# Two merge gates read out by a side branch, and a larger backlog allowed to the RNN steps, in a three-block fp32 transformer kernel

## The reference, cut to what matters

```
h = rms_norm(x, norm_mix_pre)
proj = h @ w_in                                   # 1024 x 6216
xr, gr, q, k, v, iq, ik, iw, g_a, g_b = split(proj)
xc = causal_depthwise_conv(xr, conv_w, conv_b)    # 4 taps
y_rnn = rg_lru(xc, ...) * gelu(gr)                # gates by 64-wide blocks, a scan over the 256 rows
y_a = y_rnn @ w_rnn_out
y_att = dsa_sparse_attention(q, k, v, iq, ik, iw) # 16 heads, the 64 best keys of each row
y_b = y_att @ w_att_out
merged = sigmoid(g_a) * y_a + sigmoid(g_b) * y_b
x = x + rms_norm(merged @ w_o, norm_mix_post)
...                                               # a feed-forward layer, then two more layers
```

## Time and profile before

| what | value |
|---|---|
| median of 3 runs | 1549.5 us |
| lowest and highest of them | 1546.7 and 1559.98 us |
| profiled execution, its own time | 1560.4 us |
| its span, first to last instruction | 1558.6 us |
| PE busy | 1457.6 us, 94% of the span |
| DVE busy | 908.4 us, 58% |
| ACT busy | 742.0 us, 48% |
| mean granted TensorE clock | 0.95 of full |

### The profile page before, as it was taken

How to read it: one execution, slowest core, us unless ns; L and a number is a source line. 1 busy time by engine, 2 the same in 40 slices (tenths; PEclk the granted TensorE clock), 3 DMA queues, 4 the chain that set the end, 5 groups by cost and what they waited for, 6 DMA issues and landing times.

```text
span 1558.6 us, 18397 instructions
## 1 busy us (share of the span) xinstructions
PE 1457.6 (94%) x7100; PEld 1218.9 (78%) x7100; DVE 908.4 (58%) x1445; ACT 742.0 (48%) x1120; POOL 8.1 (1%) x18
## 2 busy tenths in 40 slices
PE   7999799899998999999877999999999929999999
PEld 6898687688887888887656888888888827888887
DVE  5775686565454654547756545555555692565453
ACT  4557674454443544445434444444444525654442
POOL 1000000000000000000000000000000000000000
PEclk9999599999999999999887999999999966999999
DMA  8454055455564556554413565565555420265652
GB/s 264 150 148 122 0 167 185 149 189 178 187 202 149 165 173 202 190 163 150 133 54 100 188 199 176 193 195 180 176 196 190 124 81 1 82 192 172 202 190 68
DMA packets 131767, 242.57 MB, mean 156 GB/s; under 512 B 8544, under 2 KB 21472, under 8 KB 131680
## 3 DMA queue, kind: packets, MB, share of 16 engines
q1 hardware_dynamic: 130768, 239.15, 47.4%
q0 software_dynamic: 624, 2.10, 0.5%
q10 hardware_dynamic: 288, 0.14, 0.0%
HBM read 240.31 MB, written 1.05 MB: 155 GB/s over the span
## 4 chain that ended last, share of the span: by engine, by line
PE 89%; DVE 7%; ACT 2%; issue 1%; DMA 0%; SPq 0%; DVEq 0%
PE PB L449 78%; PE PB L477 3%; PE PB L614 2%; PE PB L679 2%; PE PB L665 1%; PE PB L604 1%; DVE WL L396 1%; DVE SM L536 1%; ACT SR L633 0%; PE PB L1064 0%; DVE SM L522 0%; DVE SM L521 0%; DVE SM L520 0%; DMA X<-in_x_dram 0%; PE PB L578 0%
## 5 line engine op out<-in xcount | busy, mean ns | idle before, releaser
L396 DVE TENSOR_TENSOR WL<-RAW,WH 128x1024 fp32r<-128x1024 f32 (+1 forms) x453 | 534.7, 1213 | 240.3 <-ACT WH L406 240.1
L406 ACT ACTIVATE WH<-RAW 128x1024 fp32r<-128x1024 f32 (+1 forms) x453 | 468.0, 1054 | 331.3 <-PE PB L449 321.1
L449 PE MATMUL PB<-WH,AT0h 128*128 128x512 f32 (+2 forms) x1328 | 510.0, 384 | 16.3 <-DVE WL L396 8.0
L449 PE MATMUL PB<-WL,AT0h 128*128 128x512 f32 (+2 forms) x1328 | 503.3, 379 | 0.0
L449 PE MATMUL PB<-WH,AT0l 128*128 128x512 f32 (+2 forms) x1328 | 502.8, 379 | 0.0
L449 PEld LDWEIGHTS PB<-WH,AT0h 128*128 128x128 f32 x1328 | 255.0, 192 | 64.8 <-ACT AT0h L489 7.0
L449 PEld LDWEIGHTS PB<-WH,AT0l 128*128 128x128 f32 x1328 | 255.0, 192 | 46.1
L449 PEld LDWEIGHTS PB<-WL,AT0h 128*128 128x128 f32 x1328 | 255.3, 192 | 43.3
L449 PE MATMUL PB<-WH,FTh 128*128 128x512 f32 x440 | 174.0, 395 | 0.0
L449 PE MATMUL PB<-WH,FTl 128*128 128x512 f32 x440 | 172.5, 392 | 0.0
L449 PE MATMUL PB<-WL,FTh 128*128 128x512 f32 x440 | 170.8, 388 | 0.0
(11 more groups left out here) (288 smaller groups left out, 1182.8 us busy)
## 6 DMA issues: line engine op xcount, KB each, us to landing
RAW<-in_ffn_w_gu_dram SPq DMA_DIRECT2D x88, 512.0 KB, 4.5
RAW<-in_ffn_w_gu_2b_dram SPq DMA_DIRECT2D x88, 512.0 KB, 4.6
RAW<-in_w_in_dram SPq DMA_DIRECT2D x48, 512.0 KB, 4.0
RAW<-in_ffn_w_down_dram SPq DMA_DIRECT2D x44, 512.0 KB, 4.0
RAW<-in_ffn_w_down_2b_dram SPq DMA_DIRECT2D x44, 512.0 KB, 3.7
RAW<-in_w_ffn_gate_dram SPq DMA_DIRECT2D x22, 512.0 KB, 4.6
RAW<-in_w_ffn_up_dram SPq DMA_DIRECT2D x22, 512.0 KB, 4.7
RAW<-in_w_ffn_down_dram SPq DMA_DIRECT2D x22, 512.0 KB, 4.5
```

What stands on the lines that cost most here:

```text
L396: e.tensor_tensor(o, s, h, ALU.subtract), th, loaded[i], hl_free[i % NHL])
L406: th = op("act", lambda e, o=WH[i % NHL][:, 0:m], s=RAW[i % NRAW][:, 0:m]: e.activation(o, s, ACT.Copy), loaded[i], hl_free[i % NHL])
L449: e.matmul(o, l, r, start=s, stop=p, skip_group_check=feature_major)
```

## The change

It does four things.

1. The read-outs of the four gate products become a generator, `merge_gate`. It is put at the head of `side` and waits there until `conv` (or `gates`) is complete. The main line goes on to the next product at once.
2. Where nothing can go on without the read-outs, the main line waits for all eight of them (`while len(kga) < 4 or len(kgb) < 4`), just ahead of `drain(*rnn_side)`.
3. Since unread gate products now hold banks (two each), `product` first waits, by `onward`, until at least four banks are in the free list. This is in force for all products of the kernel.
4. The RNN's steps wait with `calm(5.0)` in place of `calm(1.5)`, in nine places.

```diff
@@ product
                 nb = n // 128 if feature_major else 2
+                while not carry and len(banks) < 4:
+                    onward()
                 mine = carry or [take() for _ in range(nb // 2 if feature_major else nb)]
@@ rnn, and likewise at its other eight steps
-                    yield from calm(1.5)
+                    yield from calm(5.0)
@@ main line
-            for c in range(2):
-                got_g = product("w_in", 4168 + c * 512, 512, at0, 8)
-                while len(conv) < 4:
-                    onward()
+            def merge_gate(got_g, dst, c, past, toks):
+                while len(past) < 4:
+                    yield
                 for b, (bank, tok) in enumerate(got_g):
-                    kga = op("act", lambda e, b=b, c=c, bank=bank: e.activation(
-                        GA[:, b, c * 512:c * 512 + 512], PB[bank][:, :], ACT.Tanh, scale=0.5), tok, conv)
-                    give(bank, kga)
-            for c in range(2):
-                got_g = product("w_in", 5192 + c * 512, 512, at0, 8)
-                while len(gates) < 4:
-                    onward()
-                for b, (bank, tok) in enumerate(got_g):
-                    kgb = op("act", lambda e, b=b, c=c, bank=bank: e.activation(
-                        GB[:, b, c * 512:c * 512 + 512], PB[bank][:, :], ACT.Tanh, scale=0.5), tok, gates)
-                    give(bank, kgb)
+                    k = op("act", lambda e, b=b, c=c, bank=bank: e.activation(
+                        dst[:, b, c * 512:c * 512 + 512], PB[bank][:, :], ACT.Tanh, scale=0.5), tok, past)
+                    give(bank, k)
+                    toks.append(k)
+
+            kga, kgb = [], []
+            for c0, dst, past, toks in ((4168, GA, conv, kga), (5192, GB, gates, kgb)):
+                for c in range(2):
+                    side.insert(0, merge_gate(product("w_in", c0 + c * 512, 512, at0, 8), dst, c, past, toks))
+            while len(kga) < 4 or len(kgb) < 4:
+                onward()
             drain(*rnn_side)
```

## The result

| | kernel before | changed kernel |
|---|---|---|
| median, runs side by side | 1556.05 us (9 runs) | 1539.35 us (9 runs) |
| lowest and highest | 1546.7 and 1559.98 us | 1535.47 and 1540.71 us |
| profiled execution, its own time | 1560.4 us | 1539.6 us |
| its span | 1558.6 us | 1537.8 us |

The ratio is 0.9896, with a 95% interval of 0.9871 to 0.9921: the change makes the kernel some 16 us faster, by 8 to 13 thousandths (16.7 us by the medians). The forecast was 18.3 us less, from 1549.5 us. With six more runs the median of the kernel before is itself 6.5 us higher than the one that the prediction started from, so the absolute time is 8 us above the forecast, though the step down is nearly as large as forecast.

What follows compares the result with a forecast made beforehand. No engine bounds the bare stretch: two chains run alone while PE's main line stands still, losing 24.3 us. 24.3 - 2.5 - 1.5 - 2 = 18.3 us less than 1549.5 gives 1531.2 us; range 1524 to 1545 us.

Steps and rivals of the forecast that it cites:

- the bare stretch: 151.2 to 192.2 us, nothing dense in PE's queue: waiting and half clock, with the echo behind, lose 24.3 us.
- the read-outs as a branch: Gate products: dense matmuls follow each other, attention's second half moves into `w_rnn_out`, and all 24.3 us can go.
- the larger backlog: RNN steps: convolutions written five chunks earlier; weight copies and attention steps queue behind up to 5 us of RNN work.
- seam term: Between gate products and `w_rnn_out`: RNN's last pair, 29 us, done in time against 36; 1.5 us of waiting (0 to 4).
- the second rival: RNN's last pair late, so the wait returns before `w_rnn_out`: 25 us there, no gain, 1549.5 us within 3; chance 0.08.
- New waits: Three places in the stage where PE would wait instead: 2.5, 1.5 and 2 us, taken off the 24.3 us.
- at the end: Attention's last unit, right ahead of its result's transposes: PE idle in copy and scaling, 2.5 us (1.5 at least, up to 5).
- scattered waits: Small waits all along the stage, where an estimate is a little too early: 2 us, bounds 0.5 and 8.
- the clock case: `w_rnn_out` mixed with attention runs at 1.2 GHz, its 43 us take 86: slower, 1574 us; chance 5%.
- The rest of the span should be the same: Sign for the profile: outside the stage that the change touches, nothing in the span differs.
- carry the difference over as it is: Whole kernel: the median's 10.9 us below the profiled execution kept unexplained, so the forecast starts from 1549.5 us.
- the case of the new waits: Rival: late attention steps stall dense work in `w_rnn_out`, at seam and end; 7 us less, 1542 us (3 to 14); chance 0.20.

Runs made afterwards that it cites:

- The branch alone: Changed kernel with calm(1.5) in place of calm(5.0), read-outs as a branch and guard of four banks kept: 1554.26 us, ratio 1.0002.
- the backlog alone: Kernel before with calm(5.0) in place of calm(1.5) in all nine RNN steps, main line and products as they were: 1539.77 us, ratio 0.9919.
- calm(3.0): Changed kernel with calm(3.0) in place of calm(5.0), branch and guard kept: 1546.6 us, ratio 0.9958.

## Why the prediction was right, and where it was not

**The size of what is lost in the bare stretch: right.** 24.3 us were to go. In the profiles the stage lost 19.5, and 1.8 us of new waits stand in their place; 3.0 us are left. It holds for this execution: in the other two profiles of the kernel before the stage is 2.9 us shorter, so 16.6 us would have gone.

**What removes it: wrong.** "So the PE work of the stretch is unchanged, and all 24.3 us can go" stands under the read-outs as a branch. The branch alone gave a ratio of 1.0002, the backlog alone all of the gain. So the mechanism of the forecast failed, and the right size is in part luck: both parts were in the change, and it made no difference to the sum which of them was named. The step that failed beside it is the one on the larger backlog, "Its cost is that ...": it was costed, and never asked what it gives. The rows of the order had shown it: the last convolution stands five weight chunks earlier on ACT, and it is `calm` that sets where a convolution is written. With `calm(1.5)` my own seam term, "29 us against 36", would have been wrong as well, since the RNN's pair then starts late: the second rival's wait at the seam came true there, with 11.8 us in place of its 25. In the full change it didn't, as reckoned, because the RNN was ahead.

**New waits: mis-sized.** 6 us (2.5 at the end, 1.5 at the seam, 2 scattered) were 1.8: 1.1 us at the end (0.69 and 0.39), 0.7 us in two waits for QT (0.47 and 0.25), both in the last 2.6 us before the seam. The waits at the end and at the seam were forecast in their places and too large; even the "1.5 us at least" at the end was too much. The 2 us of scattered waits, with 8 us as their bound, were not there at all.

**A term that was missing: switching.** The sum took each small group by its price and each dense matmul by 0.231 us. PE's timeline of the changed kernel, at one of the cuts into `w_rnn_out`:

```profile
197.58 0.41 PE L606 MATMUL PB<-ID,QKI 128*64 128x128 f32 x2
197.75 0.48 PE L451 MATMUL PB<-WH,AT1h 128*128 128x512 f32 x1
198.07 0.40 PE L451 MATMUL PB<-WL,AT1h 128*128 128x512 f32 x1
198.30 0.39 PE L451 MATMUL PB<-WH,AT1l 128*128 128x512 f32 x1
...
199.32 0.48 PE L616 MATMUL PB<-KT,QT 64*128 64x256 f32 x1
```

The first dense matmul behind small ones takes 0.32 us to the next one's start in place of 0.23. The whole piece lasts 1.74 us, by the prices it should be 2 x 0.0875 + 6 x 0.231 = 1.56: 0.18 more. The changed kernel has 34 such groups in the stage and before had 21; 13 more at 0.1 to 0.2 us each are an estimated 1.3 to 2.6 us of the 3.0 that were left. This was worked out, no experiment isolated it.

**The clock: right, on a row that was cut short.** It stayed at 1.00 in all of the stage, in a queue cut into groups of six dense matmuls. The rule of the Trainium skill's section "A second HAM failure mode: psum-queue depth-cycling" ("TensorE: Matmul & The Clock Gate"), that frequent micro-idles make the clock go back and forth, didn't show there. That is no test of it: PE was idle only four times in the stage, 1.8 us in all. The prediction set against the rule, a window at 1.00 with 19% idle. The next window of the same kernel has a fall of the clock in it, just behind 780 us:

```profile
780.00:800.00 20.00, 18.25 (x79) 13.70 (x77) 10.56 (x24) 7.91 (x22) 0.00 (x0) 0.91 0.36 105
```

So the earlier trace rows were weaker evidence than the prediction took them for, and they are all that it names against the clock case. In the stage of the other kernels, the clock fell with the branch alone where PE stood still for 4.3 and 7.5 us, and in calm(3.0) behind 4 us of small matmuls and a wait, with nothing dense among them.

**"The rest of the span should be the same": right for this pair of profiles** (19.5 of 20.8 us), by the luck that both have the long form in the third layer. The sentence "nothing in the stage explains that, so I carry the difference over as it is" was the step that put the time wrong. The changed kernel's profiled execution lies 0.25 us above its median, not 10.9, and with nine runs that of before lies some 4 us above. A hint was at hand, the 66 of the clock line. The three runs given had two near 1549 and one at 1560; the median of them, 1549.5, was low by 6.5 us against nine. The forecast time of 1531.2 us inherits this. As a time, 1539.35 us lies outside the 1526 to 1536 us that had 0.62, in the case of the new waits, which didn't come true; as a step down, 16.7 us lies inside the forecast's 14 to 23. That the whole range of 1524 to 1545 us held the result is due to its width.

**Signs named in advance.** `w_rnn_out` lasts 47.9 us (forecast 43 to 49). The idle time ahead of L667 and L681 is 0.7 us (under 3). The wait before L479 is 0.4 us (forecast 1 to 3, too much). The transposes come 19.6 us earlier (some 18).

## What to carry to other kernels

When a main line waits for a side branch, first look at what rate that branch is let on, before the wait itself is moved: making the wait a branch of its own moved it to the next consumer and gave nothing, and one number in the branch's throttle gave everything. Try the parts of a combined change apart, since a right total doesn't show that the reasons are right. Where PE's clock line has a low digit behind an idle time, a few useless dense matmuls late in it can be worth much for their size (12 of them gave 10.3 us here, the change itself 16), and until that is settled, a difference of 0.6% between kernels, the 9.5 us here, may be the two forms of one stretch.

## What the runs showed of the hardware

- A stretch of small fp32 matmuls behind 20 us of idle time ran in two forms, 54.7 to 54.9 us and 45.0 to 45.4 us, with the clock at 0.50 for more than 20 us or soon at 1.00, and once between them (51.8 us). PE's row is nearly full in all. The same work, shifted by a few us, changed form, and not in one direction. How the moment decides is open.
- 12 dense matmuls of 512 columns right ahead of it opened the clock each time it was profiled (three kernels, 43.5 us in all of them), with no delay, as they lie in idle time.
- With the clock held at 1.00 in the bare stretch, by 60 useless matmuls, the stage took 157.1 us, against 160.6 and 157.7 us in profiles without them, and the kernel was no faster that could be measured.
- The same bare stretch of the same kernel was throttled more in one execution than in the next (stage 160.6 and 157.7 us), and with less throttling PE waited longer in it (13.1 us of idle time in the stage in place of 10.3).
